# Sixteen of twenty-four conditioning blocks computed on VectorE from transposed weights instead of on TensorE

## The reference, cut to what matters

```python
def trunk_layer(x, cvec, rope, ctx_kv, lp):
    mod = jnp.einsum('bd,de->be', jax.nn.silu(cvec), lp['w_ada']) + lp['b_ada']
    sh1, sc1, gt1, sh2, sc2, gt2 = jnp.split(mod[:, None, :], 6, axis=-1)
    h = rms_norm(x, lp['norm1_g']) * (1 + sc1) + sh1
    proj = h @ lp['w_in']                      # q, k, v, pool input, gate a, gate b
    ...                                        # attention, pooling, gates
    x = x + gt1 * (merged @ lp['w_out'])
    h2 = rms_norm(x, lp['norm2_g']) * (1 + sc2) + sh2
    x = x + gt2 * hierarchical_moe(h2, ...)
```

## Time and profile before

| | |
|---|---|
| median of 3 runs | 1691.71 us (1690.93 to 1692.45) |
| span of the profiled execution, first to last instruction | 1689.1 us |
| TensorE matmul busy | 1574.7 us (93%) |
| VectorE busy | 908.4 us (54%) |
| ScalarE busy | 658.9 us (39%) |
| GpSimd busy | 289.5 us (17%) |

### The profile page before, as it was taken

The page is one execution under the profiler, slowest core; times in us unless marked ns, Lnnn a source line. Parts: engine busy times, 40 slices in busy tenths (PEclk is TensorE's granted clock), DMA queues, the critical chain, the costliest instruction groups (busy, mean ns, idle before and its releaser), DMA issues.

```text
span 1689.1 us, 23023 instructions
## 1 busy us (share of the span) xinstructions
PE 1574.7 (93%) x8677; PEld 1307.9 (77%) x8677; DVE 908.4 (54%) x1384; ACT 658.9 (39%) x896; POOL 289.5 (17%) x214
## 2 busy tenths in 40 slices
PE   4899999999999889999999999999999499999985
PEld 3688888878888758888888888887887388888852
DVE  6471000006656348778877763334454767767627
ACT  5212112132222355656555642111222157676633
POOL 1021111112322500000100000000000125555520
PEclk9999999999999999999999999999899599999997
DMA  9143333230011010000400024327003179999965
GB/s 375 73 147 135 142 146 143 84 128 25 29 46 44 20 72 1 0 0 1 165 0 0 32 89 153 134 85 236 27 38 137 61 225 265 272 274 271 251 141 233
DMA packets 52316, 198.40 MB, mean 117 GB/s; under 512 B 8218, under 2 KB 17290, under 8 KB 40992
## 3 DMA queue, kind: packets, MB, share of 16 engines
q1 hardware_dynamic: 42016, 172.31, 28.3%
q0 software_dynamic: 10240, 25.28, 7.4%
HBM read 155.98 MB, written 44.62 MB: 119 GB/s over the span
## 4 chain that ended last, share of the span: by engine, by line
PE 45%; DMA 6%; DVE 5%; ACT 2%; issue 2%; POOL 1%; SPq 1%; POOLq 0%; DVEq 0%; ACTq 0%
PE psum L1507 8%; PE psum L1463 5%; PE psum L1637 4%; PE psum L1577 4%; PE psum L1658 3%; DMA xg<-h2d,x_row 3%; PE psum L1449 2%; PE psum L1446 2%; PE psum L1447 2%; PE psum L1432 2%; PE psum L1434 2%; PE psum L1433 2%; PE psum L1641 2%; PE psum L1586 2%; DMA y_sum<-yst,y_row 2%
## 5 line engine op out<-in xcount | busy, mean ns | idle before, releaser
L346 PE MATMUL psum<-h_hi,w_hi 128*128 128x512 f32 (+1 forms) x768 | 201.1, 370 | 10.1 <-DVE h_lo L759 5.5
L346 PE MATMUL psum<-h_lo,w_hi 128*128 128x512 f32 (+1 forms) x768 | 193.2, 360 | 0.0
L346 PE MATMUL psum<-h_hi,w_lo 128*128 128x512 f32 (+1 forms) x768 | 192.7, 359 | 0.0
L346 PEld LDWEIGHTS psum<-h_hi,w_hi 128*128 128x128 f32 x768 | 129.0, 191 | 39.1 <-issue 18.7
L1972 DVE TENSOR_TENSOR pT_lo<-psum,pT_hi 128x512 fp32r<-128x512 f32 x192 | 126.3, 686 | 51.0 <-ACT pT_hi L1740 50.7
L346 PEld LDWEIGHTS psum<-h_hi,w_lo 128*128 128x128 f32 x768 | 128.4, 189 | 23.0
L346 PEld LDWEIGHTS psum<-h_lo,w_hi 128*128 128x128 f32 x768 | 128.4, 189 | 23.0
L1740 ACT CAST pT_hi<-psum 128x512 fp32r<-128x512 f32 x192 | 104.7, 590 | 88.1 <-PE psum L1463 87.9
L656 POOL TENSOR_TENSOR w_lo<-w_raw,w_hi 128x1024 fp32r<-128x1024 f32 x32 | 77.0, 2409 | 340.4 <-ACT w_hi L520 340.4
L1463 PE MATMUL psum<-ident,prob 128*128 128x128 f32 x768 | 112.1, 276 | 2.9 <-DVE pT_lo L1972 2.5
L1463 PEld LDWEIGHTS psum<-ident,prob 128*128 128x128 f32 x768 | 93.0, 142 | 27.4 <-DVE pT_lo L1972 7.9
(11 more groups left out here) (345 smaller groups left out, 2970.5 us busy)
## 6 DMA issues: line engine op xcount, KB each, us to landing
gu_raw<-in_w_gu SPq DMA_DIRECT2D x32, 1024.0 KB, 5.4
ada<-in_w_ada SPq DMA_DIRECT2D x20, 1024.0 KB, 4.8
w_raw<-in_w_in SPq DMA_DIRECT2D x16, 1024.0 KB, 4.8
dn_raw<-in_w_dn SPq DMA_DIRECT2D x16, 1024.0 KB
gates<-gst SPq DMA_DIRECT2D x14, 640.0 KB, 2.9
y_sum<-stage SPq DMA_DIRECT2D x12, 512.0 KB, 5.0
xt<-in_x SPq DMA_DIRECT2D x10, 512.0 KB, 6.8
merged<-gates SPq DMA_DIRECT2D x8, 640.0 KB, 3.9
```

Source lines behind the costliest of these rows:

```text
L346: mm = pe.matmul(psum[:, par_sets[j] + g:par_sets[j] + g + w], a[j][:, k, :], b[:, k, g:g + w], start=(k == 0 and a is w_hi and b is h_hi) ...
```

## The change

The last sixteen blocks of `w_ada` are laid out anew on the host: outputs on the partitions, `w_adaT` as [16, 128, 2, 1024], so that a block holds, for each partition, two outputs and all 1024 weights of each. The two SiLU'd vectors are written to DRAM (`csd`) from a VectorE copy `csq`, and read back into `cs_rows`, both vectors in full on every partition (1 MB). For each block VectorE does four multiply-and-sum operations of 128x1024 (two outputs, two vectors), whose products go to `ada_junk` and whose sums to `ada_sum`, and adds the bias. The hooks of `project` go, and with them the copies and the turns of these blocks. The first eight blocks stay as they are. On SP, the store of `csq` stands ahead of the seventh block's load, and the load of `cs_rows`, which waits for the last `h_lo`, ahead of `wpool` and `icnt`; a block's buffer is free when VectorE is through with it.

```diff
--- before.py
+++ after.py
@@ -124,6 +124,9 @@
...
         ada = [at(f"ada{j}", [P, KC, PAIR], F32, RKV + (40 + 8 * j) * KB) for j in range(2)]
+        adaT = [at(f"adaT{j}", [P, 2, D], F32, RKV + (40 + 8 * j) * KB) for j in range(2)]
+        cs_rows = at("cs_rows", [P, 2, D], F32, RKV + 20 * KB)
+        ada_junk = at("ada_junk", [P, D], F32, RS)
         ada_raw = [at(f"ada_raw{j}", [P, KC, PAIR], F32, RHL + o * KB) for j, o in enumerate((20, 60, 30, 70))]
...
@@ -132,6 +135,8 @@
...
         sel = at("sel", [P, QUAD], F32, RS + KB)
+        csq = at("csq", [P, 2, KC], F32, RS + KB + 128)
+        ada_sum = at("ada_sum", [P, 2, 2], F32, RS + 4 * KB)
         sq_junk = at("sq_junk", [P, D], F32, RHL)
...
@@ -160,7 +165,7 @@
...
         s = {}
-        for n in ("eps_r x_ss rs_used consts rope wpool_in icnt_in x_sq x_scaled xT_ps xT_outa xT_outd c_in c_sig c_silu fa_mm fa_rows fa_turn fa_mods ada_mm0 ada_mm1 ada_rows0 ada_rows1 ada_turn mods_r0 mods_r1 ada_in0 ada_in1 "
+        for n in ("eps_r x_ss csq_r csd_st csd_in rs_used consts rope wpool_in icnt_in x_sq x_scaled xT_ps xT_outa xT_outd c_in c_sig c_silu fa_mm fa_rows fa_turn fa_mods ada_mm0 ada_mm1 ada_in0 ada_in1 "
                   "mods_b h_raw h_hi_r h_lo_r w_in0 w_hi0 w_hi1 w_lo0 w_lo1 mm0 mm1 ps_free0 ps_free1 pad0 xp_in xp_used "
...
@@ -212,6 +217,9 @@
...
                         sp.dma_start(w_raw[:], io["w_in"][0]).then_inc(s["w_in0"], 16)
+                    if i == 5:
+                        sp.wait_ge(s["csq_r"], 1)
+                        sp.dma_start(io["csd"].rearrange("q (p k) -> p q k", p=P), csq[:]).then_inc(s["csd_st"], 16)
 
...
@@ -221,11 +229,14 @@
...
                         sp.wait_ge(s[f"ada_mm{j}"], n - 4)
-                    sp.dma_start(ada[j][:], io["w_ada"][bass.ds(2 * n + j, 1)].rearrange("o p k n -> p (o k) n")).then_inc(s[f"ada_in{j}"], 16)
+                    sp.dma_start(adaT[j][:], io["w_adaT"][bass.ds(2 * n + j - 8, 1)].rearrange("o p m k -> p (o m) k")).then_inc(s[f"ada_in{j}"], 16)
 
...
                 load_ada(4, 1)
+                sp.wait_ge(s["csd_st"], 16)
+                sp.wait_ge(s["h_lo_r"], KC)
+                sp.dma_start(cs_rows[:], io["csd"].rearrange("(o q) k -> o q k", o=1).broadcast_to([P, 2, D])).then_inc(s["csd_in"], 16)
                 sp.wait_ge(s["xT_ps"], TILES)
...
@@ -316,20 +327,6 @@
...
 
-                def ada_block(n, j):
-
-                    pe.wait_ge(s[f"ada_in{j}"], 16 * (n - 3))
-                    if j:
-                        pe.wait_ge(s["ada_rows0"], n - 3)
-                    else:
-                        pe.wait_ge(s["ada_rows1"], n - 3)
-                    vector_times(ada[j]).then_inc(s[f"ada_mm{j}"], 1)
-
-                def ada_turn(n, j):
-                    pe.wait_ge(s[f"ada_rows{j}"], n - 3 + j)
-                    pe.wait_ge(s[f"mods_r{1 - j}"], n - 3)
-                    turn_rows(ada_rows[j]).then_inc(s["ada_turn"], 1)
-
                 def project(n, j, hooks={}):
...
@@ -381,10 +378,10 @@
...
                     for j in range(2):
-                        project(n, j, hooks={4: lambda: ada_block(4, j), 7: lambda: ada_turn(4, j)})
+                        project(n, j)
                 with pe.Fori(0, GATE_PAIRS) as i:
                     for j in range(2):
-                        project(i + G0, j, hooks={4: lambda: ada_block(i + 5, j), 7: lambda: ada_turn(i + 5, j)})
+                        project(i + G0, j)
 
...
@@ -714,6 +711,7 @@
...
                 own.step(nc.vector.tensor_copy(cs32[:, :, 0:2], cs[:]))
+                nc.vector.tensor_copy(csq[:], cs[:].rearrange("p k q -> p q k")).then_inc(s["csq_r"], 1)
                 dve.wait_ge(s["consts"], 32)
...
@@ -789,14 +787,16 @@
...
 
-                def loop_rows(n, j):
-                    dve.wait_ge(s[f"ada_mm{j}"], n - 3)
-                    rows_out(j).then_inc(s[f"ada_rows{j}"], 1)
-
-                def loop_mods(n, j):
-                    dve.wait_ge(s["ada_turn"], 2 * (n - 4) + j + 1)
-                    own.step(turned_mods(bass.ds(4 * n + 2 * j, 2)))
-                    dve.sem_inc(s[f"mods_r{j}"], 1)
+                def ada_block(n, j):
+
+                    dve.wait_ge(s[f"ada_in{j}"], 16 * (n - 3))
+                    for m in range(2):
+                        for q in range(2):
+                            own.step(nc.vector.scalar_tensor_tensor(ada_junk[:], adaT[j][:, m, :], 1.0, cs_rows[:, q, :], ALU.mult, ALU.mult,
+                                                                    accum_out=ada_sum[:, m, q:q + 1]))
+                    dve.sem_inc(s[f"ada_mm{j}"], 1)
+                    c = bass.ds(4 * n + 2 * j, 2)
+                    own.step(nc.vector.tensor_tensor(mods[:, c, :], ada_sum[:], vecs[:, c].unsqueeze(2).broadcast_to([P, 2, 2]), ALU.add))
 
...
@@ -804,8 +804,7 @@
...
                 dve.wait_ge(s["h_lo_r"], KC)
-                dve.sem_inc(s["ada_rows1"], 1)
-                dve.sem_inc(s["mods_r1"], 1)
+                dve.wait_ge(s["csd_in"], 16)
                 for c in range(4):
...
@@ -830,13 +829,11 @@
...
                     if c in (1, 2):
-                        loop_rows(4, c - 1)
-                        loop_mods(4, c - 1)
+                        ada_block(4, c - 1)
                 with dve.Fori(0, GATE_PAIRS) as i:
-                    own.enter(i, 2)
+                    own.enter(i, 10)
                     for j in range(2):
-                        loop_rows(i + 5, j)
-                        loop_mods(i + 5, j)
+                        ada_block(i + 5, j)
                     own.leave(GATE_PAIRS)
...
@@ -2411,7 +2408,8 @@
...
         "ident": np.eye(P, dtype=np.float32),
-        "w_ada": pairs(a["w_ada"][0]), "w_in": c(w_in),
+        "w_ada": c(pairs(a["w_ada"][0])[:8]), "w_in": c(w_in),
+        "w_adaT": c(a["w_ada"][0].reshape(KC, P, N_ADA, 2, P).transpose(2, 4, 3, 1, 0).reshape(N_ADA, P, 2, D)[8:]),
         "w_merge_a": columns(a["w_branch_a"][0]), "w_merge_b": columns(a["w_branch_b"][0]), "w_out": c(a["w_out"][0].reshape(KC, P, D)),
...
@@ -2437,7 +2435,7 @@
...
         io[name] = nc.dram_tensor(name, shape, f32, kind="ExternalOutput").ap()
-    for name, shape in (("gates", (2 * KC, P, TOK)), ("poolT", (4, P, TOK)), ("rows", (14 * KC, P)), ("h2d", (TOK, D)), ("y_sum", (TOK + 2 * P, D))):
+    for name, shape in (("gates", (2 * KC, P, TOK)), ("poolT", (4, P, TOK)), ("rows", (14 * KC, P)), ("csd", (2, D)), ("h2d", (TOK, D)), ("y_sum", (TOK + 2 * P, D))):
         io[name] = nc.dram_tensor(name, shape, f32).ap()
...
```

## The result

The changed kernel takes 1666.45 us (median of 4 runs, 1662.78 to 1667.31) against 1691.56 us: a ratio of 0.9842, with a 95% interval of 0.9825 to 0.9858. That is 25.1 us less, where 27.6 were forecast. The profiled execution has a span of 1664.3 us. Two more sets of runs of the same kernel, on two chips, gave 0.9836 (0.9809 to 0.9864) and 0.9840 (0.9824 to 0.9855), that is 26.8 and 27.4 us less than the kernel before beside them; the forecast, 1664.1 of 1691.71, is 0.9837.

A forecast was written before the change was run, and what follows sets the result against it. TensorE was taken to bound the conditioning stage: 16 x 1.63 = 26.1 us for blocks and turns plus 1.5 at the loop's end, 27.6 off 1691.71, gives 1664.1 us. Range 1662.5 to 1666 (0.78), wider 1661.0 to 1670.0.

The forecast's parts named there:

- TensorE sets the pace, so what leaves its queue is won: Projections of pairs 1 to 8: TensorE is busy 30.00 of 30 us, so shed work shortens the stage, 27.6 us.
- Block 1.18, turn 0.45: TensorE's cost per conditioning block (16 matmuls) and turn (4 small matmuls), in us; sixteen of both make 26.1 us.
- The gap at the end, with ScalarE free just in time: Loop's end: TensorE's wait for `mods_b` goes, 1.53 us; ScalarE, free at 340.34, is wanted at 340.55.
- VectorE's products: Four multiply-and-sum operations per block at 1.52 us, 6.3 us a block, hidden beside TensorE's period of 14.07 us.
- Crossing with GpSimd: GpSimd's low halves of the weights may lengthen one product per block by some 2.2 us: 8.5 us, still hidden.
- b: VectorE's time for one conditioning block, forecast at 6.3 us.
- the rival of half rate: Each product takes 2.57 us, a block 10.6; weights of pairs 3 and 4 come late, 5.8 us lost: 1669.9 us, chance 0.09.
- The start, margins 12 and 6.5 us: Pooling and first blocks: weights of pairs 2 and 3, behind other loads on SP, still come 12 and 6.5 us early.
- VectorE as the bound, from b = 13.6: Rival, chance 0.04: VectorE's chain passes the present 339.3 us at that block time; with 14.0 about 1697 us.
- 120.9 + 16 b: End of VectorE's chain in one piece: 101 + 9.2 + 10.7 us through the pooling, then sixteen blocks.
- The whole time: Whole kernel: 1664.1 us from 1691.71; 1662.5 to 1666 at 0.78, wider range 1661.0 to 1670.0.
- one of my own signs of being wrong: Listed signs: TensorE idle ended by `w_lo` or `mods_b`, products above 2.4 us, late pooling, a later stage over 1 us longer.

The follow-up runs named there:

- thrice: The changed kernel with every multiply-and-sum of blocks 8 to 23 done three times, same result: 1764.57 us, ratio 1.0409.
- no_turns: The kernel before, without the sixteen turns and the waits for them; block matmuls and VectorE's copies stay: 1684.79 us, ratio 0.9961.
- no_blocks: The kernel before, without the matmuls of blocks 8 to 23; turns, copies and loads stay: 1682.77 us, ratio 0.993.

## Why the prediction was right

- *TensorE sets the pace, so what leaves its queue is won.* Right. The stage shrank by 27.74 us, forecast 27.6, and it is the same with and without the products on VectorE. The last projection's closing groups start at 313.70, which is 311.9 without the late start of 1.8; the forecast had 312.
- *Block 1.18, turn 0.45.* 16 x 1.18 = 18.9, measured 19.02; 16 x 0.45 + 1.53 = 8.7, measured 8.65. The distances of the starts gave the right prices, where busy times (1.07 and 0.50) would have given 25.1 for the sixteen pairs instead of 26.1, and a wrong split.
- *The gap at the end, with ScalarE free just in time.* Right: ScalarE's cast ends at 316.35, and its first scaled product starts at 316.52, 1.06 us behind TensorE's start of 315.46. There is no margin left here.
- *VectorE's products.* 1.225 and 0.08 us, 1.27 from one to the next, where I took 1.52: a term set too high, hidden either way. The Trainium skill's rule of half throughput ("Vector Engine (DVE) Microarchitecture Reference", section 7) does not show in these traces, although both sources are fp32 in SBUF and the sum is written: by that rule the estimate is 2.57 us, twice the plain form's 1.284. A block that GpSimd doesn't meet takes 5.5 us from one closing sum to the next (142.61 to 148.13), not 6.3.
- *Crossing with GpSimd: up to 2.2 us for one product in a block.* Right in size, 3.31 against 1.23 us, 2.1 more, but not once per block: only 4 of the 64 products of the changed kernel were lengthened, to 3.0 to 3.3 us. I left it out of b, and out of the pooling, in the rival of half rate. With the low clock behind each wait, which I left out too, that is why this rival was priced too low: 5.8 us forecast, 13.8 measured with the products doubled (a stand-in for half rate, not half rate itself).
- *The start, margins 12 and 6.5 us.* `cs_rows` landed in 4.7 us, the first pooled sum was not held up by it (87.11, behind a wait for ScalarE's `xpad`), and the weights of pair 2 were issued at 93.80. Those of pair 3 were issued at 125.54 in an execution that started 1.8 us late (123.2 forecast). `w_lo` for them was done at 134.85 + 2.50 = 137.4 against the 144.7 at which pair 3 began (88.37 and four projections of 14.08), 7.3 us to spare.
- *VectorE as the bound, from b = 13.6.* Not the case here, and the mechanism holds. With the doubled products and the other order on SP, b is 12.7 on average, between the two thresholds of 11.9 and 13.6: `m2` is done at 324.5, behind the 312 and ahead of the 339.3, and the stage is still shorter than before. At 17.9 (thrice) the forecast's sum, 120.9 + 16 b, gives 407 us, and VectorE was through at 406.2. TensorE's last wait there is the one named, for `mods_b`.
- *The whole time.* 2.4 us above the forecast in the first set, inside the range of 1661.0 to 1670.0 but 0.45 above the narrower 1662.5 to 1666 to which I gave 0.78. The other two medians, 1667.32 and 1666.52, lie above 1666 as well. The first profile has them as 1.8 at the start, 1.3 in the query stage, and the rest, both ways, behind it; in other executions they are elsewhere. The three ratios, 0.9836 to 0.9842, lie around the 0.9837 of the forecast. But the three gains, 25.1, 26.8 and 27.4 us, are all below the stage's 27.74, and one of my own signs of being wrong did show: a later stage longer by more than 1 us, the query stage by 1.31 and the experts by 2.64. For the experts the kernel before was the exception: 345.92 us in its one profile, and 348.6 and 348.8 in no_turns and no_blocks, which are edits of it. For the query stage it stays open: 272.31 and 272.35 us in before and no_turns, 272.8 to 273.7 in all five profiles of the changed stage with that part unedited, so some 0.5 to 1.4 us may belong to the change. That the ratio fits the forecast so closely is in part luck; what the runs show is the stage.

## What to carry to other kernels

Where one engine is full and its work is a chain of alike groups, take the price of an insertion from the distance of the starts around it, and subtract the undisturbed step: it came out to 0.1 us in 19. Before work is moved to an idle engine, find its last consumer and write down the moved chain from its start to that consumer, with every load that stands behind its reloads in an ordered queue; here the change has 7 us of margin there, and doubling the moved work used up that margin and made the stage 13.8 us longer. After one limit is lifted, look for the next one at once: doubled products cost the same with either order of the queue, for different reasons.

## What the runs showed of the hardware

- The multiply-and-sum of two fp32 operands in SBUF, 128x1024, takes 1.225 us in 60 of 64 cases, less than the same instruction with a scalar from SBUF and no sum (1.284); reading out the sum is an instruction of 0.08 us that overlaps the end of the product.
- A product that starts while GpSimd's subtraction of 2.4 us is under way takes 3.0 to 3.3 us in the changed kernel (2.9 to 3.5 with the products doubled), so it loses most of that operation's time. GpSimd's own was lengthened too where VectorE was ahead: 2.86 and 3.19 us beside blocks 8 and 9, against 2.41 for both without the products. The prediction had counted on both (GpSimd's margin of 9.5 us that becomes 7.9). Timeline of POOL, changed kernel:

```profile
103.89 2.86 POOL L653 TENSOR_TENSOR w_lo<-w_raw,w_hi 128x1024 fp32r<-128x1024 f32 x1 [11.97 <-ACT w_hi L517]
117.97 3.19 POOL L653 TENSOR_TENSOR w_lo<-w_raw,w_hi 128x1024 fp32r<-128x1024 f32 x1 [11.22 <-ACT w_hi L517]
```

- After an idle time of 5.5 us TensorE runs at the lower of its two clock levels (0.50 of full clock) for a time that differs between executions of one program: in two profiles of the changed kernel the first groups start at 39.24 and 38.98 us, and the clock has risen by 45 and by 43 us. Of the 1.27 us between their starts of pair 1, 0.26 are there ahead of these groups, and some 1.0 comes after.
